# Router chain, unread products and seat tables moved around the expert stage of a two-block float32 transformer kernel on one Trainium2 core

## What is computed

```python
def grouped_moe(x, w_router, b_router, w_gate, w_up, w_down):
    scores = softmax(xt @ w_router + b_router)
    grp = scores.reshape(-1, 4, 4)                     # 16 experts in 4 groups
    g_sel = argmax(sum(top_k(grp, 2)[0], axis=-1))     # one group for each row
    top_w, top_i = top_k(in_grp, 2)                    # two experts in that group
    gate = one_hot(eid, 16) * top_w / sum(top_w)
    for e in range(16):
        h = silu(xt @ w_gate[e]) * (xt @ w_up[e])      # 1024 -> 512
        y = y + gate[:, e:e + 1] * (h @ w_down[e])     # 512 -> 1024
```

## Time and profile before

| what | value |
|---|---|
| median of three runs | 2280.56 us (2277.51 to 2281.64) |
| profiled execution, its own time | 2278.92 us |
| its span | 2277.1 us |
| TensorE busy (share of the span) | 2220.8 us (98%) |
| VectorE busy | 1612.7 us (71%) |
| ScalarE busy | 1286.8 us (57%) |
| GpSimd busy | 57.9 us (3%) |
| read from HBM, mean rate | 487.40 MB, 215 GB/s |

### The profile page before, as it was taken

The page is one execution under the profiler, slowest core; times in us unless marked ns, Lnnn a source line. Parts: engine busy times, 40 slices in busy tenths (PEclk is TensorE's granted clock), DMA queues, the critical chain, the costliest instruction groups (busy, mean ns, idle before and its releaser), DMA issues.

```text
span 2277.1 us, 31229 instructions
## 1 busy us (share of the span) xinstructions
PE 2220.8 (98%) x13248; PEld 1916.0 (84%) x13248; DVE 1612.7 (71%) x1577; ACT 1286.8 (57%) x1360; POOL 57.9 (3%) x71
## 2 busy tenths in 40 slices
PE   8999999999999999999999999999999999799997
PEld 7888989788888889897888998887777998687775
DVE  6765855777477557466774666589999666689997
ACT  5434644554344446445543544578887555488885
POOL 1000100000000001000000000000000000100000
PEclk9999999999999999999999999999999999899999
DMA  7755443455555554434664555479998554399995
GB/s 243 218 186 169 148 139 126 163 186 187 193 174 185 188 180 134 152 129 164 199 191 168 181 185 185 141 283 384 385 382 330 181 185 167 131 338 383 388 374 198
DMA packets 309952, 490.93 MB, mean 216 GB/s; under 512 B 15504, under 2 KB 205120, under 8 KB 309808
## 3 DMA queue, kind: packets, MB, share of 16 engines
q1 hardware_dynamic: 305712, 475.35, 61.2%
q0 software_dynamic: 3104, 10.38, 1.6%
q10 hardware_dynamic: 992, 3.15, 0.4%
HBM read 487.40 MB, written 1.44 MB: 215 GB/s over the span
## 4 chain that ended last, share of the span: by engine, by line
PE 78%; DVE 10%; DMA 7%; ACT 3%; issue 2%; DVEq 0%; SPq 0%; ACTq 0%
PE PS L807 14%; PE PS L734 14%; PE PS L730 14%; PE PS L731 13%; PE PS L810 7%; DVE RL L2203 5%; DMA RINGS<-w_down 4%; DMA RINGS<-w_gate 3%; PE PS L1422 2%; ACT RH L1662 2%; PE PS L1419 2%; PE PS L1042 1%; PE PS L1007 1%; PE PS L981 1%; PE PS L992 1%
## 5 line engine op out<-in xcount | busy, mean ns | idle before, releaser
L2203 DVE TENSOR_TENSOR RL<-RINGS,RH 128x2048 fp32r<-128x2048 f32 x448 | 1011.3, 2272 | 421.5 <-ACT RH L1662 419.5
L1662 ACT ACTIVATE RH<-RINGS 128x2048 fp32r<-128x2048 f32 x447 | 848.6, 1900 | 453.2 <-PE PS L734 375.3
L807 PE MATMUL PS<-HTS,RH 128*128 128x512 f32 x1384 | 416.3, 397 | 1.2 <-DVE HTS L2189 1.2
L730 PE MATMUL PS<-RH,HTS 128*128 128x256 f32 (+1 forms) x1184 | 342.2, 305 | 0.4 <-DVE HTS L2185 0.4
L731 PE MATMUL PS<-RH,HTS 128*128 128x256 f32 (+1 forms) x1184 | 336.1, 300 | 0.0
L807 PEld LDWEIGHTS PS<-HTS,RH 128*128 128x128 f32 x1384 | 249.7, 189 | 48.7 <-issue 1.6
L810 PE MATMUL PS<-HTS,RL 128*128 128x256 f32 x1408 | 283.3, 281 | 0.0
L734 PE MATMUL PS<-RL,HTS 128*128 128x256 f32 (+1 forms) x1184 | 261.5, 299 | 0.0
L810 PEld LDWEIGHTS PS<-HTS,RL 128*128 128x128 f32 x1408 | 228.9, 188 | 15.2
L730 PEld LDWEIGHTS PS<-RH,HTS 128*128 128x128 f32 x1184 | 223.8, 189 | 11.9 <-issue 2.5
L731 PEld LDWEIGHTS PS<-RH,HTS 128*128 128x128 f32 x1184 | 224.7, 190 | 7.2
(11 more groups left out here) (463 smaller groups left out, 2969.3 us busy)
## 6 DMA issues: line engine op xcount, KB each, us to landing
RINGS<-w_in SPq DMA_DIRECT2D x64, 1024.0 KB, 5.3
RINGS<-w_gate SPq DMA_DIRECT2D x64, 1024.0 KB, 9.3
RINGS<-w_up SPq DMA_DIRECT2D x64, 1024.0 KB, 9.4
RINGS<-w_down SPq DMA_DIRECT2D x64, 1024.0 KB, 9.1
RINGS<-ffn_w_up SPq DMA_DIRECT2D x44, 1024.0 KB, 5.3
RINGS<-ffn_w_down SPq DMA_DIRECT2D x44, 1024.0 KB, 4.9
RINGS<-ffn_w_gate SPq DMA_DIRECT2D x43, 1024.0 KB, 5.4
RINGS<-w_out SPq DMA_DIRECT2D x16, 1024.0 KB, 4.9
```

Of the source, the lines that this page charges most:

```text
L730: mm(dst, a_[0], b_[0], start=start, stop=False)
L807: return mm(PS[:, bank + c, :], wh[:, k, c * P:(c + 1) * P], HTS[:, :, k, :], start=(k == 0), stop=(k == K - 1))
L1662: A(splits.buffer(RH, RH3)[:, 0:width], RINGS[:, slot, 0:width], ACT.Copy).then_inc(wh_ready, 1)
L2203: TTn(RL[:, slot, 0:width], RINGS[:, slot, 0:width], splits.buffer(RH, RH3)[:, 0:width].bitcast(F32), ALU.subtract).then_inc(wl_ready, 1)
```

## The change

- GpSimd no longer computes XL; VectorE does (`rows_rest`), the first half ahead of the router chain, the second after the one-hot rows.
- In layer 1 VectorE no longer splits a weight chunk ahead of the router chain. ScalarE rounds the second half of the rows before its own split instead of after it.
- In layer 1 TensorE runs products whose results nobody reads: three of 512 columns before the transposes, three after `rt_ready`, one after `pos_ready`.
- VectorE's `gates`, the SEATG tables and the seat tables of groups 1 to 3 go behind the flag's branch. The gates stand after the first split, the tables in expert 0, after its second split. One gate chunk is split before `gathered(0)` and the second after it, in both layers.
- TensorE's `seat_tables` go from expert 0 to expert 1, after its first gate chunk, and ScalarE's `seats` go there as well.
- The other branch (flag 1) gets the gates alone.

```diff
@@ gpsimd
-                    if k == 2:
-                        for t in range(T):
-                            pool.wait_ge(xh_ready, T * l + t + 1)
-                            nc.gpsimd.tensor_tensor(XL[t], X[:, t, :], XH[:, t, :].bitcast(F32), ALU.subtract).then_inc(xl_ready, 1)
@@ tensor
+                def idle_products(bank, count):
+
+                    for _ in range(count):
+                        mm(PS[:, bank, :], IDENT, CON[:, O_MB:O_MB + 512], start=True, stop=True)
+
                 splits.enter()
                 if l == 0:
                     unit_ahead(11, 2)
+                else:
+                    idle_products(3, 3)
...
                 last.then_inc(rt_ready, 1)
                 if l == 0:
                     unit_ahead(12, 5)
+                else:
+                    idle_products(5, 3)
...
                 mm(PS[:, 4, 40:80], CON[:, O_ONE:O_ONE + P], both, start=True, stop=True).then_inc(pos_ready, 1)
                 if l == 0:
                     unit_ahead(13, 2)
+                else:
+                    idle_products(5, 1)
...
                         stacked(0, 0, j)
+                        if e == 1:
+                            seat_tables()
                         if j == 0:
...
                         folded(0, e, CORG, 1)
-                        if e == 0:
-                            seat_tables()
-                        else:
+                        if e:
                             pe.wait_ge(eh_l, l * NE + e)
@@ scalar
                 rows_rounded(0)
                 ht_copy(tr2(l, 3), HT)
-                split(back=3)
+                rows_rounded(1)
                 chunk()
                 A(RLT, PS[0:2 * NE, 4, 0:S], ACT.Copy).then_inc(rt_cols, 1)
                 A(EPS[:, 1:2], EPS[:, 0:1], ACT.Exp)
                 act.wait_ge(rt_in, l + 1)
                 A(SMALL[:, 256:288], SMALL[:, 256:288], ACT.Exp).then_inc(rt_exp, 1)
-                rows_rounded(1)
+                split(back=3)
...
                         chunk()
                         split(back=3)
+                        if e == 1:
+                            seats()
                         chunk()
                         rests(e, CORG, 0)
...
                         if e == 0:
-                            seats()
                             return
@@ vector
                     ht_copy(tr2(l, 3), HT)
                     ahead.experts = ahead.n
-                    split()
-
+
+                def rows_rest(t):
+                    dve.wait_ge(xh_ready, T * l + t + 1)
+                    TTn(XL[t], X[:, t, :], XH[:, t, :].bitcast(F32), ALU.subtract).then_inc(xl_ready, 1)
+
+                rows_rest(0)
                 ring.n += 1
                 dve.wait_ge(rt_ready, l + 1)
...
+                rows_rest(1)
                 dve.wait_ge(oh_ready, l + 1)
                 dve.wait_ge(pos_ready, l + 1)
...
                 TSc(CROWDED, SMALL[:, 500:501], SEATS + 0.5, None, ALU.is_gt).then_inc(crowd_known, 1)
-                gates()
-                for t in range(T):
-                    TTn(SEATG[:, :, t, :], spread(CON[:, O_NTH:O_NTH + P], 1, NG_), spread(PLACE[:, t, 0:NG_], 2, P), ALU.is_equal)
-                for g in range(1, NG_):
-                    last = expert_seats(g)
-                last.then_inc(seat_ready, 1)
                 wait_apart(dve, crowd_known, l + 1, consts_loaded, 16 * NLOAD)
...
                         split()
+                        if e == 0:
+                            seat_tables()
                         if e:
                             hidden_low(e - 1, 7)
...
-                    split()
-                    if l == 0:
-                        split()
+                    def seat_tables():
+                        for t in range(T):
+                            TTn(SEATG[:, :, t, :], ...)
+                        for g in range(1, NG_):
+                            last = expert_seats(g)
+                        last.then_inc(seat_ready, 1)
+
+                    split()
+                    gates()
                     gathered(0)
+                    split()
                     for e in range(NE):
```

More of the change, by code:

```diff
@@ L2853, in gates @@
                     for t in range(T):
-                        TTn(GATE[:, :, t].rearrange("p (g i) -> p g i", i=4), SMALL[:, 416 + 16 * t:432 + 16 * t].rearrange("p (g i) -> p g i", i=4),
-                            spread(SMALL[:, 468 + 4 * t:472 + 4 * t], 2, 4), ALU.mult)
+                        last = TTn(GATE[:, :, t].rearrange("p (g i) -> p g i", i=4), SMALL[:, 416 + 16 * t:432 + 16 * t].rearrange("p (g i) -> p g i", i=4),
+                                   spread(SMALL[:, 468 + 4 * t:472 + 4 * t], 2, 4), ALU.mult)
+                    link(last)
                 if l == 0:
@@ L2954, in seated @@
                         ring.n += 6 if e else 4
+                    def seat_tables():
+                        for t in range(T):
+                            TTn(SEATG[:, :, t, :], spread(CON[:, O_NTH:O_NTH + P], 1, NG_), spread(PLACE[:, t, 0:NG_], 2, P), ALU.is_equal)
+                        for g in range(1, NG_):
+                            last = expert_seats(g)
+                        last.then_inc(seat_ready, 1)
                     split()
-                    if l == 0:
-                        split()
+                    gates()
                     gathered(0)
+                    split()
                     for e in range(NE):
@@ L2976, in _ @@
                     add_residual(1, PS[:, 6:8, :].rearrange("p b n -> p (b n)")).then_inc(mean_ready, 1)
-                    sparse, paired = steps.n - apart, NE + T
+                    sparse, paired = steps.n - apart, NE + T + 3
                     assert sparse <= paired
@@ L2989, in dense @@
                         expert(e, T, GCUR, left, more)
-                    dve.wait_ge(seat_ready, 2 * l + 2)
-                    if l == 0:
-                        split()
+                    gates()
+                    dve.sem_inc(seat_ready, 1)
+                    split()
                     split()
```

## The result

The changed kernel takes 2283.14 us, the median of 20 runs (2276.14 to 2287.57), against 2277.71 for the kernel before (20 runs, 2274.84 to 2281.64). The ratio is 1.0018, 95% interval 1.001 to 1.0027: some 4 us slower, where no change was forecast. Each ratio is to the kernel before on the same occasion: beside a_fill, b_chain, c_tables and f_back the kernel before had a median of 2278.86 us, beside d_noidle, e_pool and g_fill one of 2278.53, so medians of different experiments are not to be subtracted. One run of a_fill took 4373.48 us; no trace shows why, and it is left out of the ratio.

The account below looks back on a forecast made before the run. Bound: the moment DMA transfers become continuous, plus the bytes left. Layer 0 +1.2 and layer 1 -1.85, together -0.65 on the median of three runs: 2279.9 us, called no change; range 2272.5 to 2286.5.

Parts of the forecast that it names:

- then the tables, 8.03: Expert 1, behind its first gate chunk: TensorE's seat tables take 8.03 us, their first 4 us at full clock.
- a rival at 0.12: TensorE's clock halves between expert 0's end and the seat tables in one layer: +3.8 us, 2283.7 in all; chance 0.12.
- F6 - G: Both layers: from gathered(0)'s end on VectorE to the sixth free slot's load issue; 24.55 us forecast, 20.2 before.
- X to F6: From VectorE starting the last norm rows to sixth free slot's load; 1.65 us more in layer 0, 1.4 less in 1.
- the credit for the fifth load: Five loads instead of four precede the transfer hole, which then ends at the sixth slot: -0.45 us a layer.
- The comparison beside GpSimd: Router chain: a VectorE comparison taking 2.32 us beside GpSimd's subtraction drops to near 0.17, 2.15 sooner.
- Place product of layer 1: VectorE's place product, behind the router chain and second subtraction, comes 3.65 us earlier, at 1976.7.
- Unread products: Layer 1: filling TensorE's gaps keeps full clock, gather(0) takes 4.0 us instead of 6.72; chance they fail 0.09.
- G: End of gathered(0)'s four low parts on VectorE: 5.75 us earlier in layer 1, 2.7 in layer 0.
- Branch 1.0: The branch after the crowd flag, ahead of VectorE's first split, no longer hidden by queued work: 1.0 us.
- The rival of 3.8: The branch after the crowd flag costs 3.8 us instead of 1.0: 2284.5 in all; chance 0.08.
- The rival in which the waits are hidden: TensorE isn't held in experts 0 and 1, so F6 - G stays at 20.2 us: 2271.2 in all; chance 0.18.

Follow-up runs that it names:

- a_fill: Changed kernel with three more unread products in each layer, in TensorE's waits between expert 0's end and the seat tables: 2277.21 us, ratio 0.9998.
- b_chain: Changed kernel with gates, tables, seat tables and seats back where they stood; router chain, unread products and single split kept: 2274.56 us, ratio 0.9981.
- c_tables: Kernel before with only the gates, tables and seat tables moved as in the change: 2283.17 us, ratio 1.0021.
- f_back: Changed kernel with TensorE's seat tables and ScalarE's seats back in expert 0, VectorE's tables left where moved: 2282.71 us, ratio 1.0017.
- d_noidle: Changed kernel without the seven unread products of layer 1: 2281.61 us, ratio 1.001.
- e_pool: Changed kernel with the XL subtraction back on GpSimd instead of VectorE: 2284.71 us, ratio 1.0023.
- g_fill: b_chain plus unread products: two behind gather(0) of layer 1, one amid each layer's two-column products: 2277.76 us, ratio 0.9995.
- again1: Changed kernel, unchanged, profiled a second time: 2277.70 us.
- again2: Changed kernel, unchanged, profiled a third time: 2278.33 us.

## Why the prediction was wrong

**The step that failed** is "then the tables, 8.03", with the chances put on it. The tables were taken at full clock in their first 4 us in both layers (0.40), and a fall ahead of them in one layer was a rival at 0.12. In the profiled execution layer 1 takes 11.7. That its F6 - G is 4.73 above the forecast splits up, by the rows of after and again1, into 3.5 in the tables (11.7 against 8.2, start to start), 0.8 in the four products before them and 0.4 in the chunk after; the rival's price was 3.8.

The rival had the price, but not its condition: it charged 3.8 for any fall ahead of the tables. Of seven such layers five cost at most 1.2 above the forecast, and two, in which the clock fell in the last wait before the tables, 4.7. Where it never fell ahead of them the forecast held: in again1 X to F6 is 1.3 more than before in layer 0 and 1.95 less in layer 1 (forecast, without the credit for the fifth load: 1.65 more and 1.4 less), -0.6 together, at 2277.7 us.

All three are outcomes of one program. Of its 20 runs 6 took less than 2280, two 2280.0 and 2280.4, and 12 took 2281.96 to 2287.57; the three whose mean granted clock is 0.994 lie at 2276.1 to 2279.4, the eight at 0.991 or less at 2282.95 to 2287.57. The median belongs to the larger group. That the larger group is runs with tables at half clock in a layer is shown by a profile only at 2284.25 us; for the others it is inferred from time and mean clock, from a_fill, which fills the waits and is back at 0.9998, and from e_pool, whose profiled execution (2285.8) has the same 29.28.

That the measured 2283.14 lies close to the 2283.7 of this rival is partly luck. The forecast stood on 2280.56, the median of three runs; twenty runs of the same kernel give 2277.71. From there the forecast is 2277.1 and the rival's case 2280.9. With the measured 4.7 instead of 3.8 it would be 2281.8. The ratio (4 us slower than before) fits that, the median lies 1.3 above it; how many of the runs have the late fall, and whether some have it in both layers, isn't shown.

The reasoning behind the low chance was that layer 0 had kept its clock over an idle stretch of 2.68 and layer 1 had lost it after one of 3.07, so that 2.1 and 1.2 seemed short. They were shorter still, 1.40 and 0.42, with one of 0.45 ahead of them that the forecast doesn't have. What stood ahead of the tables was this string of short waits around 512-column work, and the same string ends in more than one way. A single row on each side of such a limit was no ground for 0.12.

**What held, by the prediction's steps.**
- The comparison beside GpSimd: 0.19 (forecast 0.17), GpSimd silent. e_pool brings the stall back, so the reason holds too.
- Subtraction 1.15: measured 1.22. Place product of layer 1: 10.67 after X against 14.80, 4.1 sooner (forecast 3.65).
- Unread products: gather(0) of layer 1 at full clock, pairs of 0.40, as in layer 0; d_noidle has 0.63 and G 2.2 later.
- Branch 1.0: measured 0.85 in layer 1 and 1.09 in layer 0. The rival of 3.8 is out, and the rule of the Trainium skill ("Runtime: NRT & Kernel Launch", Instruction fetch mechanics) has at most the size of that row here: the idle time isn't divided into read, decision and fetch, and which of them it is stays open.
- G: -6.3 and -3.1 (forecast -5.75 and -2.7).
- F6 - G = 24.55: right in layer 0 (24.55), in again1 (24.58, 24.56), in layer 1 of again2 and in layer 0 of c_tables (24.57). Layer 1 of c_tables has 24.5 by another way, with the clock down ahead of the tables. The rival in which the waits are hidden is out: no kernel with the tables behind e1's first chunk has less than 23.1.
- The fifth load, -0.45 a layer: not told apart. The rest of the span moves by up to 2 us from one profiled execution to the next, in both directions.

**The sum of the parts.** The chain with its single split is worth -0.19% (b_chain); the moved tables alone cost +0.21% (c_tables). The full change, +0.18%, isn't their sum, +0.02%. X to F6 says where it parts: b_chain is 4.9 us below before, c_tables 4.2 above, -0.6 together, and that is what the full change has in again1 (-0.6); in the execution with the late fall it has +4.1. So the two halves add up as long as the clock isn't lost in the last wait before the tables. That the shorter chain of the full change is what tips it isn't shown: again1 has the same chain and keeps its clock, and e_pool, with a chain 1.35 longer in layer 1, loses it.

The best version measured is b_chain, 2274.56 us. VectorE makes its tables while TensorE gathers, and in the rows above, TensorE doesn't wait for them at the end of expert 0.

## What to carry to other kernels

Small table work that cost 8 us between full chunks cost 8.6, 9.1 or 12.0 at the end of a string of waits of 0.4 to 1.4 us, in one and the same program; before moving such work, see what TensorE does just ahead of its new place. Where a step's clock can go either way, forecast two times and not one, profile more than one execution, and read the spread of the runs: 11.4 us for the changed kernel, 4.4 for b_chain, which has no such waits ahead of its tables. Products nobody reads paid in the waits right ahead of the tables (a_fill), brought G forward but no time that could be told ahead of gather(0) (d_noidle), and didn't pay amid the two-column products (g_fill).

## What was unexpected of the hardware

- One program, with waits equal within 0.04 us, had TensorE at 1.2 GHz throughout the tables in one execution and at 2.4 GHz for the first of them in two others (1.90 against 3.51 for L1505).
- The clock also falls with TensorE never idle: in b_chain, with no wait ahead, the 32 two-column products took 3.68 us in layer 0 and 4.05 in layer 1, in layer 1 the granted clock was 0.99 from 1999 to 2000 us and 0.50 from 2000 to 2001 us, the last of them still running, and the chunk behind the tables began at 1.91 a group instead of 1.09. A single unread product amid them didn't hold it in layer 1 (g_fill).
- After a fall the clock came back ahead of or among the first table products where it had fallen at the start of the chunk before them, and stayed down for 11.7 us and more of them where it had fallen in the middle of that chunk (the table of twelve layers above).
- Which small VectorE operation GpSimd's subtraction holds depends on when they meet: L2811 in the kernel before, the first two-operand one of the chain in e_pool. GpSimd is held too: its two subtractions take 4.75 us in layer 1, 2.4 each as in the earlier trace rows, and 7.06 in layer 0, where a VectorE split of 2.28 runs beside them.
- TensorE's wait of 1.40 for Silu in e1 is mostly a load of ScalarE's function table. Its timeline after, layer 1:

```profile
1996.45 1.28 ACT L2108 ACT_TABLE_LOAD   x1
1997.74 0.59 ACT L2108 ACTIVATE Y<-PS 64x512 f32<-64x512 f32 x1
```

Loading it earlier was not tried. By an estimate from these rows (0.42 and the 1.28 saved) VectorE's split would then hold TensorE in the changed kernel, for 1.7 us instead of 0.42.
